# Two-layer decoder trunk on one core: one third of layer 0's adaLN row moves from TensorE's matmuls to VectorE's multiply-adds

## The reference, cut to what matters

```python
D_MODEL = 1024; SEQ = 256; DEPTH = 2
def reference(x, c, ada_w, ada_b, ...):
    c_act = jax.nn.silu(c)                         # (1, 1024)
    for l in range(DEPTH):
        mod = c_act @ ada_w[l] + ada_b[l]          # (1, 6144)
        sh1, sc1, g1, sh2, sc2, g2 = jnp.split(mod, 6, axis=-1)
        h = rms_norm(x) * (1.0 + sc1[:, None, :]) + sh1[:, None, :]
        y = even_mixer(h, ...) if l % 2 == 0 else odd_mixer(h, ...)
        x = x + g1[:, None, :] * y
        h = rms_norm(x) * (1.0 + sc2[:, None, :]) + sh2[:, None, :]
        x = x + g2[:, None, :] * hier_moe(h, ...)  # 32 experts, top 2
    return x
```

## Time and profile before

| | before |
|---|---|
| median of 3 runs | 1389.27 us (1388.14 to 1389.96) |
| the profiled execution | 1389.08 us, span 1387.3 us |
| TensorE (PE) busy | 1257.4 us, 91% of the span |
| VectorE (DVE) busy | 428.5 us, 31% |
| ScalarE (ACT) busy | 223.5 us, 16% |
| DMA | 493.43 MB, mean 356 GB/s |
| mean granted TensorE clock | 0.974 of full speed |

### The profile page before, as it was taken

One profiled execution on the slowest core, in us unless ns is written; L12 is line 12 of the kernel. 1 busy time (PEld: TensorE's weight loads), 2 busy tenths in 40 slices (PEclk: granted clock), 3 DMA queues, 4 the chain that ended last, 5 costly groups with the idle time before them and its releaser, 6 DMA issues.

```text
span 1387.3 us, 15049 instructions
## 1 busy us (share of the span) xinstructions
PE 1257.4 (91%) x6137; PEld 610.7 (44%) x6137; DVE 428.5 (31%) x942; ACT 223.5 (16%) x465; POOL 103.6 (7%) x127
## 2 busy tenths in 40 slices
PE   5899898899999998989898899789999889989898
PEld 2444466633443333434345456663344333433334
DVE  3474865412111211211114983441111211111112
ACT  1213332211110110101110024121110101101101
POOL 2020003001200300300000000000000000000000
PEclk9999999999999999999999999899999999999999
DMA  9983496289999999999999448528999999999995
GB/s 366 379 271 118 190 423 229 105 345 428 429 425 429 428 427 428 428 428 428 427 424 400 177 182 321 230 93 349 428 426 429 427 426 428 428 429 428 427 428 215
DMA packets 51768, 493.43 MB, mean 356 GB/s; under 512 B 4712, under 2 KB 5936, under 8 KB 20848
## 3 DMA queue, kind: packets, MB, share of 16 engines
q1 hardware_dynamic: 49104, 488.85, 84.9%
q10 hardware_dynamic: 1568, 2.68, 0.5%
q0 software_dynamic: 1024, 0.88, 0.4%
HBM read 489.24 MB, written 3.15 MB: 355 GB/s over the span
## 4 chain that ended last, share of the span: by engine, by line
PE 57%; DMA 31%; DVE 8%; issue 2%; ACT 1%; SPq 0%; POOLq 0%; ACTq 0%; POOL 0%; DVEq 0%; PEldq 0%
DMA ring<-in_moe_w 23%; PE B L825 23%; PE B L842 8%; DMA work<-in_moe_w 5%; PE A L727 4%; PE A L852 4%; PE B L639 4%; DMA ring<-in_ada_w 3%; PE B L614 3%; PE B L797 2%; PE B L578 2%; PE B L567 1%; PE B L1089 1%; PE B L655 1%; DVE hT L1209 1%
## 5 line engine op out<-in xcount | busy, mean ns | idle before, releaser
L825 PE MATMUL B<-ring,work 128*64 128x512 f32 x1648 | 442.8, 617 | 42.4 <-DMA ring<-in_moe_w 30.9
L1457 DVE TENSOR_TENSOR work<-work,B 64x512 f32<-64x512 f32 x64 | 68.2, 1065 | 647.0 <-ACT work L1848 647.0
L825 PEld LDWEIGHTS B<-ring,work 128*64 128x64 f32 x1648 | 142.4, 142 | 267.8 <-issue 266.4
L842 PE MATMUL B<-ring,work 128*64 128x512 f32 x816 | 184.7, 594 | 1.2 <-ACT work L1852 1.2
L1848 ACT ACTIVATE work<-B 64x512 f32<-64x512 f32 x64 | 37.7, 589 | 605.0 <-PE B L825 605.0
L825 PE MATMUL B<-work 128*64 128x512 f32 x272 | 123.3, 607 | 5.2 <-DMA ring<-in_moe_w 5.0
L852 PE MATMUL A<-work 128*128 128x256 f32 x512 | 118.1, 384 | 8.9 <-DVE work L1463 8.9
L842 PEld LDWEIGHTS B<-ring,work 128*64 128x64 f32 x816 | 60.9, 137 | 110.1 <-issue 109.8
L852 PEld LDWEIGHTS A<-work 128*128 128x128 f32 x512 | 94.7, 190 | 28.5 <-issue 16.9
L2097 POOL COPY work<-work 128x512 f32 x62 | 38.1, 614 | 860.0 <-PE B L825 731.2
L1463 DVE COPY work<-B 64x512 f32<-64x512 f32 x64 | 43.7, 683 | 115.4 <-PE B L842 115.4
(11 more groups left out here) (279 smaller groups left out, 1025.8 us busy)
## 6 DMA issues: line engine op xcount, KB each, us to landing
ring<-in_moe_w SPq DMA_DIRECT2D x154, 2048.0 KB, 24.9
work<-in_moe_w SPq DMA_DIRECT2D x26, 2048.0 KB, 24.9
ring<-in_ada_w SPq DMA_DIRECT2D x24, 2048.0 KB, 15.2
early<-in_moe_w SPq DMA_DIRECT2D x12, 2048.0 KB, 27.2
ring<-in_ev_w_in SPq DMA_DIRECT2D x6, 2048.0 KB, 13.5
ring<-in_od_w_in SPq DMA_DIRECT2D x4, 2048.0 KB, 18.8
ring<-in_ev_w_out SPq DMA_DIRECT2D x2, 2048.0 KB, 20.3
ring<-in_od_w_out SPq DMA_DIRECT2D x2, 2048.0 KB, 7.7
```

The costliest lines, as they stand in the source:

```text
L825: ins = pe.matmul(B5[64 * m:64 * m + 64, :], xs[:, k, :], w[:, k, :], start=(k == 0), stop=(k == KD - 1))
L842: ins = pe.matmul(B7[64 * m:64 * m + 64, :], hidTb[:, k, :], w[:, k, 512 * m:512 * m + 512], start=(k == 0), stop=(k == KF - 1))
L1457: dve.tensor_tensor(hid[64:128, :].rearrange("p (k q) -> p q k", k=KF), silu_a[64:128, :].rearrange("p (q k) -> p q k", k=KF), B5[64:128, ...
```

## The change

TensorE's `ada_rows(0, 2)` goes. VectorE multiplies each weight row of that third by the value of c that belongs to its partition and sums over the eight k in `adasum`, 128x2048 in the tile `early`. The sum over the 128 partitions is left to TensorE: four matmuls of `ones` (128x32) with `adasum` give the same bank as before. VectorE's eight operations (`ada_sum(0)` to `ada_sum(7)`) stand at these places: 0 and 1 ahead of `set_norm(0, 6, 0)`, 2 and 3 in step 0 of attention A, 4 and 5 in step 1, 6 in step 2, 7 in step 3, each time between the softmax unit of the step and the `combine_unit` of the unit before. The four loads move up in `LOADS0` among the projection chunks, so slots are given in another order; slots that held them come free by the new semaphore `ada_sums`. The counts of `slot_used` and `ada_done` are lowered to match. The rest of the diff takes out semaphores that nothing used.

```diff
-          + [("in", q) for q in range(2, 5)] + [("s5",)] + [("in", 5), ("in", 6)] + [("ada", 0, j) for j in range(8, 12)]
+          + [("in", 2), ("ada", 0, 8), ("in", 3), ("ada", 0, 9), ("ada", 0, 10), ("ada", 0, 11), ("in", 4), ("s5",), ("in", 5), ("in", 6)]
           + [("ada", 1, j) for j in range(4)] + [("out", 0), ("out", 1)])
...
+SUMMED = [LOADS0.index(("ada", 0, 8 + j)) for j in range(4)]
...
+    if n in SUMMED[1:]:
+        return LOADS0.index(("in", 4 + (n == SUMMED[3]))) + 0.3 * SUMMED.index(n)
...
+        adasum = early[:, 0:2048]
...
             if n < N_MIX1:
-                return n + (n < S5_AT)
-            return N_MOE[0] - 1 + sum(what[0] != "tab" for what in LOADS1[:n - N_MIX1 + 1])
+                return n + 1 - sum(x <= n for x in (S5_AT, *SUMMED))
+            return N_MOE[0] - 5 + sum(what[0] != "tab" for what in LOADS1[:n - N_MIX1 + 1])
...
+                if old in SUMMED:
+                    sp.wait_ge(ada_sums, 2 * SUMMED.index(old) + 2)
+                    return
...
             attention(0, 0, A_UNITS, rest_of_projections)
-            ada_rows(0, 2)
+            bank = pass_bank("ada0r2")
+            pe.wait_ge(ada_sums, KD)
+            for g in range(4):
+                ins = pe.matmul(bank[32 * g:32 * g + 32, :], ones[:, 0:32], adasum[:, 512 * g:512 * g + 512], start=True, stop=True)
+            ins.then_inc(tr_done, 1)
...
+            def ada_sum(k):
+
+                n = SUMMED[k // 2]
+                if k % 2 == 0:
+                    dve.wait_ge(slot_full[slot(n)], fills(n))
+                rows = slot_rows(n)[:, k % 2, :]
+                if k == 0:
+                    ins = dve.tensor_scalar(adasum, rows, crep[:, k, 0:1], None, ALU.mult)
+                else:
+                    ins = dve.scalar_tensor_tensor(adasum, rows, crep[:, k, 0:1], adasum, ALU.mult, ALU.add)
+                ins.then_inc(ada_sums, 1)
+                dve.wait_ge(ada_sums, k + 1)
+
+            ada_sum(0)
+            ada_sum(1)
             set_norm(0, 6, 0)
             for j in range(NA + 1):
                 if j < NA:
                     softmax_unit(0, j, *A_UNITS[j], sc_sb, prob_a)
+                for k in ((2, 3), (4, 5), (6,), (7,))[j] if j < 4 else ():
+                    ada_sum(k)
                 if j:
                     combine_unit(j - 1, *A_UNITS[j - 1][1:])
```

More of the change, by code:

```diff
@@ L310, in build @@
         ada_done, ada_copied, oa_copied = sem("ada_rows_done"), sem("ada_rows_copied"), sem("a_outputs_copied")
-        s5_slot = sem("s5_slot_free")
+        s5_slot, ada_sums = sem("s5_slot_free"), sem("ada_sums")
         sq_ready, ssq_done, var_ready, sd_ready, h_ready = (sem(n) for n in ("sq_ready", "ssq_done", "var_ready", "sd_ready", "h_ready"))
@@ L357, in build @@
         out_s = sem("out_written")
-        p5_tr, p5_dt, p5_arg, p5_sc, p5_bt, p5_lam = (sem(n) for n in ("s5_lam_T", "s5_dt", "s5_arg", "s5_sincos", "s5_bt_in", "s5_turns"))
-        ph_ready, tab_ready, bu_done, bu_read, prod_ready, y5_done, tab_used = (sem(n) for n in (
-            "phase_ready", "tab_ready", "bu_done", "bu_read", "prod_ready", "y5_done", "tab_used"))
+        p5_dt, p5_arg, p5_sc, p5_bt = (sem(n) for n in ("s5_dt", "s5_arg", "s5_sincos", "s5_bt_in"))
+        ph_ready, bu_done, bu_read, prod_ready, y5_done = (sem(n) for n in (
+            "phase_ready", "bu_done", "bu_read", "prod_ready", "y5_done"))
         tab_out = [sem(f"table_written{b}") for b in range(4)]
@@ L583, in ada_part @@
                     ins.then_inc(ada_done, 1)
-                    pe.wait_ge(ada_done, 3 * l + r + 1)
+                    pe.wait_ge(ada_done, 3 * l + r + 1 - (3 * l + r > 1))
             def ada_rows(l, r):
@@ L1974, in beside_b @@
                 if j == 5:
-                    act.wait_ge(ada_done, 4)
+                    act.wait_ge(ada_done, 3)
                     act.copy(modrow[:, :], B4[:, :]).then_inc(ada_copied, 1)
@@ L2026, in beside_c @@
                 if j == 5:
-                    act.wait_ge(ada_done, 6)
+                    act.wait_ge(ada_done, 5)
                     act.copy(modrow[:, :], B5[:, :]).then_inc(ada_copied, 1)
```

## The result

| | before | after |
|---|---|---|
| median of 6 runs, us | 1389.54 | 1398.03 |
| lowest to highest, us | 1388.14 to 1390.40 | 1395.01 to 1400.78 |
| profiled execution, us (its span) | 1389.08 (1387.3) | 1395.83 (1394.0) |
| VectorE busy, us | 428.5 | 446.7 |
| TensorE operations | 6137 | 6081 |

The ratio is 1.0054, with a 95% interval of 1.0035 to 1.0073: slower, by half a per cent. 1393.0 us was forecast, with a range up to 1396.0; the direction is right and the time is 5.0 us too low.

The account below looks back on a forecast made before the run. VectorE's queue in attention A was to become the bound, ahead of layer 0's weight-bound experts. Delay 6.5 plus head of B 1.0 less gains 3.6 made +3.9 us on 1389.08: 1393.0 us, range 1389.0 to 1396.0.

Parts of the forecast that it names:

- Rival (c): Faster: multiply-adds run at TENSOR_SCALAR's pace, 1.28 us, and nearly fit VectorE's idle time in attention A; 1386.2 us, chance 0.10.
- Sums 0 and 1 under the wait for ScalarE's root: Ahead of set_norm(0): their 3.7 us cost nothing, hidden in VectorE's 6.28 us wait.
- The hole: Attention A: TensorE stands 4.8 us for the first map near 121 us, then loses another 0.4 and 0.2 us.
- The clock: The projection behind the 4.8 us hole runs slowly, paying 1.7 us, of which 0.4 to 0.6 replace short waits.
- T: End of VectorE's normalization of the B columns, ahead of attention B; 167.16 us before the change.
- D: Delay of T through attention A: 5.4 us at TensorE's clock of before, 6.5 us with the clock loss.
- T': VectorE's first operation behind T, a place where traces are compared: 167.31 us before, 175.28 after.
- Rival (b): The same VectorE overhang in attention A without any clock loss: +1.8 us, 1390.9 us, chance 0.27.
- The head of B: Start of attention B: 1.3 us gained against T, 2.35 us from moved loads, 1.0 us lost to slow clock.
- One for one to the end: What the change does ahead of 268 us reaches the end unchanged, since layer 0's experts are bound by weights.
- Rival (d): Sums slow down beside loads writing the same ring, or the clock stays low longer in both places: +7 us, 1396 us, 0.05.
- (e): A sum waits for its load, as at the head of each slot: 1393 to 1397 us, chance 0.03.

Follow-up runs that it names:

- the one with the sums spread: Changed kernel with sum 2 ahead of step 0 of attention A and sums 3 to 7 behind the combination of steps 0 to 4: 1391.88 us, ratio 1.0002.
- the added work alone: Kernel before plus a memset and seven multiply-adds of 128x2048 on VectorE at the change's places; TensorE's third and the loads stay: 1397.90 us, ratio 1.0050.
- projection-first run: Changed kernel with TensorE's woven projection ahead of the map's transposes in steps 2 and 3 of attention A: 1398.47 us, ratio 1.0051.
- runs with padding: Small transposes at the head of TensorE's program: 56 on the changed kernel 1391.82 us; on the kernel with sums spread, 56 gave 1384.91, eight ratio 0.9966.
- the empty instructions: Changed kernel with 112 instructions that do nothing at the head of TensorE's program: 1398.37 us, ratio 1.0057.
- both edits: Changed kernel with sums spread and half of layer 1's first adaLN part ahead of attention B's last transposes: 1384.92 us, again 1383.62; ratios 0.9961, 0.9954.
- the fill alone: Changed kernel with only half of layer 1's first adaLN part moved ahead of attention B's last two transposes, the rest in steps 1 and 3: 1390.60 us.
- eight transposes: Kernel with the sums spread plus eight small transposes at the head of TensorE's program: 1387.59 us, ratio 0.9966.
- both edits and the padding: Changed kernel with sums spread, layer 1's adaLN part moved ahead of B's last transposes, and 56 small transposes at the head: 1382.60 us, ratio 0.9943.

## Why the prediction was right and wrong

**The bound and the mechanism: right.** VectorE's queue in attention A became the bound. The run without sums 2 to 7 takes the whole delay away, the one with the sums spread all but 1.0 us of it, and the added work alone brings it. The projection-first run shows that another order on TensorE doesn't shorten VectorE's queue.

**Price of the sums: right.** 2.351 us forecast as 2.33, and 1.286 as 1.28. Rival (c), which needed under 1.9 us, is out. The upper bound was reckoned wrongly: 2048 columns are 16 times 128 and not 8, so scaling the 128-column row gives 5.6 us and not 2.8; the figure that I used didn't hang on it. The Trainium skill (VectorE: DVE Perf Modes, "The perf-mode tier table") lists 2293 ns for `tensor_tensor` and 1227 ns for `tensor_scalar` on fp32 at 2048 columns. The trace is within 0.06 us of both, with the multiply-add set beside `tensor_tensor`.

**Sums 0 and 1 under the wait for ScalarE's root: right.** The wait shrank from 6.28 to 1.96 us, and attention A starts 0.3 us later, which is within what its start varies by.

**The hole: right, a little small.** 5.12 us against 4.8, then 0.40 as forecast; the third hole, of 0.2, didn't come.

**The clock: right in kind, too small.** The slow projection costs 5.94 - 3.60 = 2.3 us and not 1.7. So D is 8.0 us instead of 6.5: 0.3 from the start of attention A, 0.3 from the hole, 0.6 from the clock; the remaining 0.3 fits the short waits, of which I had counted 0.4 to 0.6 as replaced. This is the first mis-sized term. That the clock's part reaches T in full is seen in five traces with this placement of the sums: the projection behind the hole takes 5.41, 5.90, 5.94, 6.09 and 6.16 us, and from the first score to T' pass 61.9, 62.4, 62.5, 62.6 and 62.7 us. The price of 1.7 us came from a single row, and that row is no typical one. All eighteen traces have that wait of 2.65 to 2.67 us; the projection behind it took 5.29 us in the kernel before, 4.36 to 4.61 in ten others, and 3.60, without any loss, in seven. So the size was in part luck. Rival (b), without a clock loss, is out.

**The head of B: nearly right.** First score T + 4.4 (forecast 4.0), softmax T + 5.3 (5.15), the clock's part 3.00 - 1.92 = 1.1 us (1.0), waits for loads gone as forecast. From T to the out-projection the change gains 27.5 - 25.3 = 2.2 us, where my terms give 1.3 + 2.35 - 1.0 = 2.6. The Trainium skill (TensorE: Matmul & The Clock Gate, "Why this matters for your kernels") warns only of longer gaps than these, and by it this stretch would have stayed at full clock. The gaps of 2.76 and 2.09 us with the slow part behind them speak against it.

**One for one to the end: wrong.** This step failed. At the out-projection the difference was 5.7 us (forecast 3.9), which lies in what the two terms above missed; at the first pack it was 5.1. Through the experts of layer 0 the step held: from the first pack to the sums of squares of layer 1 pass 480.4 us in both traces. Behind that I had written that nothing changes, and named a difference arising after 268 us as what would prove me wrong. It did arise: 2.1 us are gained up to the last transposes, 1.7 of them at the head of layer 1, where the 2.74 us stall is gone and a 1.75 us wait for a load has taken its place, and 3.7 us are lost in the last stretch. I had the stall of 2.74 us in the trace of before and never asked what sets it. At the head of layer 1 it is partly hidden by a transfer; at the end there is nothing to hide it. The runs with padding show that its place goes with that in TensorE's program, which the removal of 56 operations shifts for everything behind it. What makes TensorE stand there stays open.

**The profiled execution.** The terms add up to the profiled 1395.83 us; the other 2.2 us to the median of 1398.03 are the spread of the changed kernel's runs, in which the profiled one lies low (with the empty instructions it lay 4.3 us low). I had equated the two, as they are 0.2 us apart for the kernel before. So of the 5.0 us missed, 1.2 arose up to the first pack, 1.6 behind it, and 2.2 lie between the profiled execution and the median.

**Rival (d)** has the time of the profiled run (1396) but not the cause: no multiply-add is slow, and the clock's two parts are together only 0.7 us above the forecast. (e) is out: no sum waits for its load.

## What to carry to other kernels

Work moved to an engine with idle time is free only if it is cut to fit each gap: six sums of 2.35 us cost 8 us where they stood ahead of the operation that another engine waits for, four of them in pairs, and about 1 us with one to a step behind it. A hole on TensorE can be paid twice, once as the wait and once as the matmuls behind it at half clock (1.8 to 2.6 us behind the hole of 5.12), so work that is ready should be put into a wait that can't be avoided. And when operations are added or removed, look in the trace for idle time put down to nothing: it can move to a place where nothing covers it, and some operations of padding (8 or 56 here) tell whether it did. The price of a stall or of a slow spell is not to be taken from one row of one trace.

## What the hardware showed that I had not expected

- **A stall of 3 us that depends on the place in the program.** It shows behind the twelfth or thirteenth sum of squares of layer 1 (2.74, 1.05, 3.01, 0.97 and 0.84 us: all five kernels with 6137 operations on TensorE), or at the last transposes (2.5 to 3.7 us: eight traces with 6081, and the one with a single one more), and in four traces at neither (both edits twice, the fill alone, eight transposes). The row of "issue" may not be all of it. In three traces a wait beside one of the two places is longer than elsewhere, though it is put down to VectorE: 4.27 us (both edits, first time) and 4.16 us (eight transposes) ahead of the sums of squares, where the rest have 2.4 to 2.7, and 1.71 us ahead of the last transposes with both edits and the padding, where the rest have 0.24 at most beside the stall itself. Both places stand shortly behind a branch of TensorE's program over the code for additional experts, which isn't executed. In the interval of the stall the DMA view shows one packet of the instruction queue, here from 1384.3 to 1387.5 us of the changed kernel:

```profile
DMA packets 1, 0.02 MB, mean 5 GB/s; under 512 B 0, under 2 KB 0, under 8 KB 0
...
q8 instruction: 1, 0.02, 2.6%
```

  That TensorE waits there for its next instructions would fit this, but such packets also land where nothing stands still, and no run has moved the branch. It is argued and not shown. Nor does the place explain everything: the kernels with the adaLN part moved have the same 6081 operations as the changed one and no such stall, and the one kernel measured twice with both edits waited 4.27 us at the head of layer 1 the first time and 2.56 the second.
- **TensorE's clock behind gaps.** Behind 5.12 us of waiting 1.8 to 2.6 us were lost (six traces), behind 3.84 us 1.7 us, behind 1.02 us none. In the pair of gaps at the head of B, of which 2.76 and 2.09 us are an instance, 0.6 to 1.7 us were lost. Behind 2.65 to 2.67 us the loss was anything from none (seven traces) to 1.7 us, so a gap's length alone doesn't tell it. With half the sums' width, for one, there was none:

```profile
151.89 0.44 PE L574 MATMUL B<-cst,htok 128*128 128x128 f32 x2 [2.67 <-DVEq L1178]
...
152.61 3.60 PE L621 MATMUL B<-ring,hT 128*128 128x512 f32 x8
```

- **56 useless transposes at the head may help by more than the stall.** With them the first score of attention A comes at 110.77 to 111.56 us, without them at 111.17 to 114.01. The granted clock over the first 45 us is 0.92, 0.92 and 0.89 with them and 0.81 to 0.92 without (0.92 in two traces: the fill alone, and both edits the second time). So whether they bring anything there isn't settled.
